# Extra identity products on TensorE at the waits of the last four stages of a one-core transformer step

## The reference, cut to what matters

```python
mixed, final_state = token_mixer(h, p, init_state)
x = layer_norm(DN_ALPHA * x + gate1 * mixed, p['ln1_g'], p['ln1_b'])
h = layer_norm(x) * (1.0 + scale2) + shift2
x = layer_norm(DN_ALPHA * x + gate2 * hier_moe(h, p), p['ln2_g'], p['ln2_b'])
...
# hier_moe: the best of 4 groups, then the best 2 of its 8 experts
hid = silu(h @ w_e1[e]) * (h @ w_e3[e])      # 1024 -> 256
out = (hid * gate) @ w_e2[e]                 # 256 -> 1024
```

## Time and profile before

| | |
|---|---|
| three timed runs | 1515.19, 1516.83, 1518.12 us |
| profiled execution | 1516.01 us, span 1514.2 us |
| PE busy | 1342.9 us, 89% of the span |
| DVE, ACT, POOL busy | 564.9, 292.1, 78.3 us |
| mean granted TensorE clock | 0.945 of full |
| memory traffic | 242.42 MB, 160 GB/s over the span |

### The profile page before, as it was taken

The page is one execution under the profiler, slowest core; times in us unless marked ns, Lnnn a source line. Parts: engine busy times, 40 slices in busy tenths (PEclk is TensorE's granted clock), DMA queues, the critical chain, the costliest instruction groups (busy, mean ns, idle before and its releaser), DMA issues. The chain is left out here.

```text
span 1514.2 us, 15851 instructions
## 1 busy us (share of the span) xinstructions
PE 1342.9 (89%) x6158; PEld 779.3 (51%) x6158; DVE 564.9 (37%) x1291; ACT 292.1 (19%) x597; POOL 78.3 (5%) x138
## 2 busy tenths in 40 slices
PE   4899999779898999899999999999947987878874
PEld 2455555455577777566777555554443332323321
DVE  5231576488023334344444520115861111111118
ACT  2202443351233224111112000000010111111110
POOL 0000000000000000000000000002001211111100
PEclk9999999889998999999999999999967999999987
DMA  9433324112002001111111218106195999999943
GB/s 376 172 139 111 112 84 167 56 35 91 6 6 89 6 6 56 64 35 56 42 42 43 63 63 264 63 21 261 42 360 218 417 420 420 419 420 420 413 165 159
DMA packets 63501, 242.42 MB, mean 160 GB/s; under 512 B 22174, under 2 KB 30942, under 8 KB 43326
## 3 DMA queue, kind: packets, MB, share of 16 engines
q1 hardware_dynamic: 57230, 229.80, 39.7%
q0 software_dynamic: 6048, 10.50, 1.8%
q10 hardware_dynamic: 144, 1.05, 0.2%
HBM read 233.54 MB, written 19.31 MB: 167 GB/s over the span
## 5 line engine op out<-in xcount | busy, mean ns | idle before, releaser
L2569 PE MATMUL bank<-ew,xgT 128*64 128x512 f32 x672 | 165.6, 650 | 48.4 <-issue 35.2
L501 PE MATMUL bank<-hT,ring 128*128 128x512 f32 x320 | 165.4, 599 | 0.0
L2569 PEld LDWEIGHTS bank<-ew,xgT 128*64 128x64 f32 x672 | 56.7, 150 | 155.1 <-issue 155.1
L1647 PE MATMUL bank<-hT,w_ab 128*128 128x512 f32 x256 | 131.2, 594 | 0.8 <-issue 0.8
L928 PE MATMUL bank<-hT,ring 128*128 128x512 f32 x192 | 98.6, 596 | 2.2 <-DVE yA L1445 2.2
L502 PEld LDWEIGHTS bank<-hT,ring 128*128 128x128 f32 x320 | 60.9, 190 | 76.4 <-issue 76.4
L2709 DVE SCALAR_TENSOR_TENSOR uh<-uh,bank 128x256 f32<-128x256 f32 x21 | 8.9, 422 | 206.8 <-ACT uh L2651 206.8
L1648 PEld LDWEIGHTS bank<-hT,w_ab 128*128 128x128 f32 x256 | 48.8, 191 | 61.1 <-issue 61.1
L2584 PE MATMUL bank<-ew,hidT 128*64 128x512 f32 x336 | 76.7, 599 | 1.2 <-ACT hidT L2645 0.6
L2086 PE MATMUL bank<-w_out,mT 128*128 128x512 f32 x160 | 70.9, 605 | 2.2 <-PEq L1580 2.2
L1762 PE MATMUL bank<-hT,w_c 128*128 128x512 f32 x128 | 65.6, 594 | 0.0
(11 more groups left out here) (439 smaller groups left out, 2100.5 us busy)
## 6 DMA issues: line engine op xcount, KB each, us to landing
ew<-in_experts SPq DMA_DIRECT2D x123, 1024.0 KB, 26.5
ring<-in_blocks SPq DMA_DIRECT2D x10, 2048.0 KB, 8.7
mhalf<-in_mods SPq DMA_DIRECT2D x16, 1024.0 KB, 5.1
w_ab<-in_merge SPq DMA_DIRECT2D x16, 768.0 KB, 4.4
mstage<-in_mods SPq DMA_DIRECT2D x3, 2048.0 KB, 18.2
w_c<-in_merge SPq DMA_DIRECT2D x8, 768.0 KB, 4.4
yt<-expert_rows SPq DMA_DIRECT2D x5, 1024.0 KB, 12.4
w_out<-in_w_out SPq DMA_DIRECT2D x1, 4096.0 KB, 12.1
```

Source lines behind the costliest of these rows:

```text
L501: pe.matmul(lat[:, :], w, hT[:, k, P:T], start=(k == 0), stop=(k == KD - 1))
L1647: pe.matmul(bank[5][:, :], w[:, k, :], hT[:, k, P:T], start=(k == 0), stop=(k == KD - 1))
L2569: mm = pe.matmul(bank[2 + n % 2][hs, :], xgT[:, n % 2, k, hs], ew1[2 * (n % 3) + h][k // 4][:, 512 * (k % 4):512 * (k % 4) + 512], start=( ...
```

## The change

A helper `filler(pe, n)` issues n products of the 128x128 identity with itself into columns 0 to 127 of bank 7. It waits for nothing and signals nothing. It is called at seven places: 10 products ahead of logits(3) and 3 ahead of logits(4) in "out"; 22 at the start of "route", 30 between "rank" and "tab", 34 behind "tab", in the route block still; 16 behind the last unit of "experts"; 12 at the start of "final". That is 127 products. No other instruction is added, removed or moved; the gathers of units 0 and 1 stand where they stood.

```diff
+    def filler(pe, n):
+
+        for _ in range(n):
+            pe.matmul(bank[7][:, 0:P], ident, ident, start=True, stop=True)
+
...
                 if i == 3:
                     pe.wait_ge(got8, 32)
+                if i == NT + 1:
+                    filler(pe, 10)
                 if i >= 3:
                     logits(i - 3)
                 if 0 <= i - 2 < NT:
                     turn(i - 2)
+                if i == NT + 1:
+                    filler(pe, 3)
...
         def _(pe):
+            filler(pe, 22)
             pe.wait_ge(v9.sem, v9.after("mall"))
...
             mm.then_inc(p9.step("rank"), 1)
+            filler(pe, 30)
             pe.wait_ge(v9.sem, v9.after("rhs2"))
...
             mm.then_inc(p9.step("tab"), 1)
+            filler(pe, 34)
...
                 ffn2(n, 1)
                 pe.nop()
+        filler(pe, 16)
...
         def _(pe):
+            filler(pe, 12)
             for t in range(NT):
                 pe.wait_ge(got_y[t], 16)
```

## The result

The changed kernel takes 1521.16 us, the median of ten timed runs (1519.58 to 1522.28), against 1516.41 us for ten of the kernel before on the same chip (1514.7 to 1518.12). The ratio is 1.0032, with a 95% interval of 1.0022 to 1.0041: slower by 4.8 us, where 4.7 us faster was predicted. It lies outside the predicted range of 1509.0 to 1516.8 us. The profiled execution has a span of 1518.9 us and a mean granted clock of 0.954 (before: 1514.2 us and 0.945). So the clock went up and the time went up with it.

The account below looks back on a forecast made before the run. Weight loads bound the experts, so starting their stream 3.3 us earlier and shortening the first sum by 1.0 gave 1516.0 - 3.3 - 1.0 = 1511.7; adding half of a 0.8 us offset gave 1512.1 us, range 1509.0 to 1516.8.

Parts of the forecast that it names:

- Step 6, the 16: Behind the last unit of "experts": they end at 1466.4, hidden by 1 us before the barrier falls.
- Step 6, the 12: Start of "final": hidden, then 2.3 us of gap; first sum 3.4 us for 5.4 if the clock holds; gain entered 1.0.
- Steps 3 and 4: In "route": the 30 keep the clock and "tab" gains 1.05 us; the 34 cost 0, with no cover left.
- Step 2: Start of "route": the 22 end 1.7 us late, "rank" then takes 1.5 us for 3.0; cost 0.2 (-0.5 to +0.9).
- Step 1: In "out": the 10 and 3 are hidden, the `h2` store holds the barrier until 1117.5; gain 0, "route" entered at 0.50.
- Step 5: Unit 0 of "experts": transposes gain 0.95 us and `ffn1` 1.5 us at full clock.
- The clock doesn't hold: Before unit 0's `ffn1` and the last sum the clock falls again: gain 1.1 us, time 1515.5; chance 0.16.
- The fetch at the entry of a block: PE, branching last into "experts", stalls on an instruction fetch: 1.7 us of 4.7 lost, time 1513.8; chance 0.09.
- Fillers at 0.50: Mainly in "route": identity products don't raise the clock, groups end late, 21.5 us more, time 1538; chance 0.06.
- a clock of 0.50 after 1125: Sign of a wrong forecast, which expected 1.00 from about 1122.5 through `ffn1` of unit 0.
- PE's filler row touching the first transposes: Sign of a wrong forecast, ahead of unit 0: fillers run up to the transposes with the rows landed long before.

Follow-up runs that it names:

- e3: Changed kernel with the bodies of PE's conditional parts for units 21 to 25 left empty, same number of tests; 1519.18 us, ratio 1.0012.
- e4: Changed kernel with PE's conditional parts of units 21 to 25 inside one outer test; 1514.10 us, ratio 0.9980.
- e7: Kernel before, no fillers, with the parts of units 21 to 25 inside one outer test on PE, ACT, DVE and POOL; 1515.47 us, ratio 0.9989.
- e1: Changed kernel without the 16 behind the last unit; 1515.36 us, ratio 0.9992.
- e2: Kernel before with only the 16 behind the last unit added; 1520.60 us, ratio 1.0030.
- e5: Changed kernel without the 16 and with 26 products in place of the 34; 1513.26 us, ratio 0.9978.
- e12: Changed kernel without the 16 and the 12, with 26 in place of the 34; 1514.46 us, ratio 0.9987.
- e11: Changed kernel without the 10 and 3, 12 for the 22, 26 for the 34, outer test for units 21 to 25 on four engines; 1515.35 us.
- e8: Changed kernel with 12 for the 22, 26 for the 34, and the outer test for units 21 to 25 on four engines; 1513.29 us, ratio 0.9974.
- e9: Changed kernel without the 16, the 10 and the 3, with 26 in place of the 34; 1512.02 us, ratio 0.9967.
- e10: Changed kernel without the 16 and with 35 products in place of the 30, the 34 kept; 1513.48 us, ratio 0.9981.

## Why the prediction was wrong

**Step 6, the 16 ("PE ends at 1462.83, they end 1466.4 ... Hidden by 1 us"): the step that failed.** It took them to start when the last product ends. The order of instructions shows them as neighbours, but between them stand 26 tests of parts that don't run, 0.16 us each (e3, e4). They cost nothing in the kernel before, where a walk of 4.1 us on PE ends at 1466.9, beside POOL's scatter and POOL's own walk, which end at 1467.8 (e4, e7). The fillers behind it make a chain of them: 4.1 us of walk, in which the clock falls, and 6.7 us at 0.50 for the 3.6 counted. Predicted 0, measured +6.2; e1 gives 5.8 of it back and e2 alone brings 4.1. Without this step the time would have been that of e1, inside the predicted range but 3.3 us above the forecast. The rows of e1's profile add to -1.65 us for the forecast -4.3. What is missing there are the 34 (1.86), the store (0.74), "rank" (0.66 beyond the forecast 0.2) and the stage of the loads (0.24); the 12 earned 0.73 more and "tab" 0.13.

**Step 6, the 12.** 0 for the predicted -1.0 in the changed kernel, where a gap of 2.03 us follows them and the clock falls 0.8 us into the sum; in e1, e5 and e12 they are worth 1.4 to 1.7 us of the sum. The mechanism is right. Whether the clock survives that gap isn't settled by its length: it fell in the changed kernel, e3 and e11 (2.03, 1.91, 2.26 us) and held in e4 and e8 (2.01, 2.21), where the 16 had run whole at 1.00.

**Steps 3 and 4: a wrong clock behind a right gain.** "Tab" gave 1.17 us for the predicted 1.05. "The wait is 8.05 us, they take 6.75: 1.3 us of gap, clock held" was wrong: the clock fell at 1137.0. It fell in eight of ten kernels with such a gap, held in e8 and e9, and held in e10 without the gap; "harmless" for gaps near 1 us was read from too few rows. So the 34 took 9.26 us and not 7.65, and the step that had said of itself "each late microsecond of the 34 is a microsecond of `ffn1`" cost 1.82 us.

**Step 2.** The 22 ended 2.5 us behind `mall`, for 1.7, since the rise came 5.7 us after their start, as with the 128x128 products of the earlier trace rows, and not 4.4. Cost 0.83 for 0.2, inside its own bounds. 12 products were enough (e8).

**Step 1.** The clock held through the logits, which the prediction had left open, and "route" was entered at 0.50, as said. But the store was awaited 8.5 us for 7.7, and "route" began 0.80 us later after it. Kernels with the two groups show 0.65 to 1.0 us more than before, e2 and e7; without them e9 and e11 have 0.1 to 0.4 more. That the cost is theirs in part is likely and not shown; why a store of SP's should land later when PE works faster stays open.

**Step 5** was right to 0.03 us, and so was the carrying-over: from the first load of unit 3 the stage took 305.3 us in both kernels.

**The rivals.** "The clock doesn't hold" described the end of "route" in part. (Its gain of 1.1 us off the median of 1516.8 gives 1515.7, where 1515.5 is written.) Its sign, a clock of 0.50 after 1125, came, and so did PE's filler row touching the first transposes. The fetch at the entry of a block didn't come: PE's first instruction of "experts" runs 0.41 us after its last filler, that of "final" 0.42 us, and a block change where PE had long waited took 0.4. By the Trainium skill, "Runtime: NRT & Kernel Launch", instruction fetch mechanics, a taken branch to code that isn't fetched yet stalls until a DMA has brought it; no row here shows it at a block's entry, and e3's profile leaves it at most 0.6 us of the walk. The stall of e11 inside straight code might be of its kind. "Fillers at 0.50" came nearest to the truth: slower, through groups that end late at the fallen clock. It was priced for all groups and given 6 in 100, because identity products do raise the clock (at 1123.3 and 1471.5). That they run at 0.50 until then was counted for the 22 and not for the 16, ahead of which no wait was seen.

## What to carry to other kernels

Before an instruction is put "into the wait" of an engine, ask when the engine's sequencer gets there: conditional parts that don't run are not free (0.16 us each on PE here), and an engine's idle time may be its walk through them. Ask also at which clock a group starts. Behind a long wait it is the fallen one, and the size must fit at 0.447 us a product until the clock rises (12 did what 22 were to do, e8). In the middle of a chain it is 1.00, but the clock may fall in a gap of 1.3 us, so the same 26 ended with the rows in e5 and 1.8 us before them in e9, where the clock fell soon after that wait. So 26 had no margin on either side. Each group that ended late cost its lateness in full. A group ahead of a barrier holds every other engine too, so it needs the widest margin, or none of it should be there: e5, which is the changed kernel with one group removed and one cut by eight, is 7.9 us faster than it.

## What was not expected of the hardware

- 26 conditional parts that don't run stood for 4.08 us on PE, 3.44 with empty bodies, and one around all of them for 0.33 us (after, e3, e4). On POOL five fewer took 0.76 us less (e7).
- Products of 78 columns ran at the full clock for 2.1 us (1134.88 to 1137.0) before the clock fell, after a gap of only 1.29 us. It held after gaps of 1.35 and 1.28 us in e8 and e9, and with a gap of 0.16 us in e10: the length of the gap alone doesn't settle it.
- A gap of 1.81 us, transposes of 1.09 and 0.89 us of idling put `ffn1` at the fallen clock (e9); with 1.54 us for the gap it stayed at 1.00 (e8). Waits for weights of 2.36 and 2.09 us let it fall (e8, e11), one of 2.10 us did not (e5).
- The last scatter landed 2.1 us after its issue in most profiles and 3.4 to 4.1 us after it in four (after, e3, e10, e12).
- PE can stand 2.73 us inside a run of products that wait for nothing (e11).
